# A two-block transformer kernel: order of splits, copy-outs, squares and gate in the second block's first projection

## What is computed

```python
h = rms_norm_2(x, norm_w[l]) * (1.0 + scale[:, None]) + shift[:, None]
proj = h @ w_in[l]
(qa, ka, va, za, beta_in, a_in, qb, kb, vb, zb, ga, gb) = jnp.split(proj, split_points, axis=-1)
qkv = causal_dwconv_silu(jnp.concatenate([qa, ka, va], axis=-1), conv_w[l])   # 4 taps
qa, ka, va = jnp.split(qkv, [DN_QK_WIDTH, 2 * DN_QK_WIDTH], axis=-1)
q_dn = l2_normalize(qa.reshape(b, s, DN_HEADS, DN_DK))       # x * rsqrt(sum(x*x) + EPS)
k_dn = l2_normalize(ka.reshape(b, s, DN_HEADS, DN_DK))
v_dn = va.reshape(b, s, DN_HEADS, DN_DV).astype(jnp.float32)
beta = jax.nn.sigmoid(beta_in.astype(jnp.float32))
g = -jnp.exp(a_log[l]) * jax.nn.softplus(a_in + dt_bias[l])
...
```

## Time and profile before

| | us |
|---|---|
| median of 3 runs | 2798.96 |
| lowest, highest | 2794.41, 2801.51 |
| span of the profiled execution | 2791.1 |
| TensorE busy in it | 2607.1 (93%) |
| VectorE busy | 1670.5 (60%) |
| ScalarE busy | 998.7 (36%) |
| GpSimd busy | 86.6 (3%) |

### The profile page before, as it was taken

One profiled execution on the slowest core, in us unless ns is written; L12 is line 12 of the kernel. 1 busy time (PEld: TensorE's weight loads), 2 busy tenths in 40 slices (PEclk: granted clock), 3 DMA queues, 4 the chain that ended last, 5 costly groups with the idle time before them and its releaser, 6 DMA issues. The chain is left out here.

```text
span 2791.1 us, 37630 instructions
## 1 busy us (share of the span) xinstructions
PE 2607.1 (93%) x15345; PEld 2208.5 (79%) x15345; DVE 1670.5 (60%) x2721; ACT 998.7 (36%) x1376; POOL 86.6 (3%) x132
## 2 busy tenths in 40 slices
PE   7999988999999999988999999989888898989997
PEld 3888877888888888856689989867778886777786
DVE  4888784467777766444447657566655653444644
ACT  4226545332212232344443323235422222334632
POOL 0100000000000000000000000021000000000000
PEclk9999999999999999999999999999989999999999
DMA  6650002223343323111034444212200000212232
GB/s 238 191 160 16 17 15 76 91 84 95 103 152 112 105 95 109 52 65 38 1 105 131 153 128 127 99 53 76 86 16 16 16 9 16 91 56 75 79 102 83
DMA packets 62109, 232.40 MB, mean 83 GB/s; under 512 B 6897, under 2 KB 9585, under 8 KB 61298
## 3 DMA queue, kind: packets, MB, share of 16 engines
q1 hardware_dynamic: 46962, 175.46, 19.1%
q0 software_dynamic: 14976, 54.53, 6.2%
HBM read 227.08 MB, written 2.10 MB: 82 GB/s over the span
## 5 line engine op out<-in xcount | busy, mean ns | idle before, releaser
L378 DVE TENSOR_TENSOR w_lo<-w_raw,w_hi 128x1024 fp32r<-128x1024 f32 (+4 forms) x284 | 348.8, 1228 | 381.8 <-ACT w_hi L337 379.2
L337 ACT ACTIVATE w_hi<-w_raw 128x1024 fp32r<-128x1024 f32 (+4 forms) x284 | 297.8, 1049 | 223.4 <-PE late_acc L459 93.4
L459 PE MATMUL mid_acc<-mid_h_hi,w_hi 128*128 128x258 f32 x832 | 279.5, 336 | 1.5 <-DVE mid_od_fq L627 1.0
L459 PE MATMUL mid_acc<-mid_h_hi,w_lo 128*128 128x258 f32 x832 | 279.0, 335 | 0.0
L459 PE MATMUL mid_acc<-mid_h_lo,w_hi 128*128 128x258 f32 x832 | 277.2, 333 | 0.0
L459 PE MATMUL late_acc<-late_h_hi,w_hi 128*128 128x258 f32 x704 | 199.3, 283 | 0.0
L459 PE MATMUL late_acc<-late_h_hi,w_lo 128*128 128x258 f32 x704 | 198.5, 282 | 0.0
L459 PE MATMUL late_acc<-late_h_lo,w_hi 128*128 128x258 f32 x704 | 197.7, 281 | 0.0
L459 PEld LDWEIGHTS mid_acc<-mid_h_hi,w_hi 128*128 128x128 f32 x832 | 157.3, 189 | 19.3 <-issue 2.4
L459 PEld LDWEIGHTS mid_acc<-mid_h_lo,w_hi 128*128 128x128 f32 x832 | 157.6, 189 | 18.6 <-issue 1.2
L459 PEld LDWEIGHTS mid_acc<-mid_h_hi,w_lo 128*128 128x128 f32 x832 | 156.9, 189 | 16.1
(11 more groups left out here) (558 smaller groups left out, 6271.1 us busy)
## 6 DMA issues: line engine op xcount, KB each, us to landing
w_raw<-in_up SPq DMA_DIRECT2D x88, 512.0 KB, 3.5
mid_side_raw<-in_ada_t POOLq DMA_DIRECT2D x48, 512.0 KB, 3.8
w_raw<-in_down SPq DMA_DIRECT2D x32, 704.0 KB, 4.0
qvz_side_raw<-in_ada_t POOLq DMA_DIRECT2D x32, 512.0 KB, 3.8
w_raw<-in_dn_qkv SPq DMA_DIRECT2D x25, 512.0 KB, 3.2
late_side_raw<-in_ada_t POOLq DMA_DIRECT2D x24, 512.0 KB, 4.0
w_raw<-in_da SPq DMA_DIRECT2D x18, 512.0 KB, 3.3
w_raw<-in_ev_qvz SPq DMA_DIRECT2D x16, 512.0 KB, 3.6
```

Of the source, the lines that this page charges most:

```text
L337: nc.scalar.activation(K.whi[:, g % 2, 0:width], K.raw[:, g % 2, 0:width], ACT.Copy).then_inc(K.hi_done, 1)
L378: nc.vector.tensor_tensor(K.wlo[:, g % 2, 0:width], K.raw[:, g % 2, 0:width], K.whi[:, g % 2, 0:width].bitcast(F32), ALU.subtract).then_in ...
L459: last = nc.tensor.matmul(self.acc[i % len(self.acc)][:, at:at + width], left[:, j, cols], right[k][:, moving:moving + width], start=(k == ...
```

## The change

The weight split moves from turn 1 to turn 0 of a tile, ahead of the copy-out (`take`, turn 0 to 1) on ScalarE and of the convolution (turn 0 to 1) on VectorE. The silu of a tile moves from its turn 5 to turn 2 of the next tile, that of the last tile to its turn 7. Sums and roots are scheduled one tile later, and the sums of slots 1 and others 2 turns earlier within it. GpSimd does the squares and, in pairs behind squares 6, 7, 10, 11, 14 and 15, also multiplies the slots by their roots, one slot (512 elements) at a time, the last four at the end; VectorE's multiplications of four slots are gone. The gate's steps on GpSimd follow squares 8, 9, 12 and 13. The gate's Exp and Ln on ScalarE stand right behind the first and second block of roots and use their table set; the reciprocal on VectorE is replaced by Exp(-Ln) on ScalarE; the gate's transposes move to tile 18.

```diff
--- before.py
+++ after.py
@@ -2554,9 +2554,10 @@
         self.ps = c.enter_context(nc.psum_tensor("dq_ps", [P, self.Q * LAT], F32))
         self.ps_t = c.enter_context(nc.psum_tensor("dq_ps_t", [P, LAT], F32))
         self.unread = c.enter_context(nc.psum_tensor("dq_unread", [P, 512], F32))[:, 0:P]
-        self.flow = Flow(K, c, "dq", w, 25, DT, h_hi, h_lo, 0, LAT, [(0, self.take), (5, self.silu)],
-                         [(0, self.convolve)], nxt, "conv0 conv1 conv2 conv3 silu_done", acc=acc,
-                         ready=ready)
+        self.flow = Flow(K, c, "dq", w, 25, DT, h_hi, h_lo, 0, LAT,
+                         [(1, self.take), (2, self.silu_before), (7, self.silu_last)],
+                         [(1, self.convolve)], nxt, "conv0 conv1 conv2 conv3 silu_done", acc=acc,
+                         ready=ready, split_turn=0)
         (self.padded, self.squared, self.total, self.logged, self.rooted, self.normed) = K.signals(
             "l2", "padded squared total logged rooted normed")
         (self.shifted, self.folded, self.tail, self.up, self.back, self.lost, self.inv, self.kept, self.ln_up,
@@ -2583,6 +2584,14 @@
         if i:
             act.wait_ge(conv3, i)
             self.nc.scalar.activation(self.dst[:, i - 1, :], self.conv[:, i % 2, :], ACT.Silu).then_inc(silu_done, 1)
+
+    def silu_before(self, act, f, i):
+        if i:
+            self.silu(act, f, i - 1)
+
+    def silu_last(self, act, f, i):
+        if i == f.n - 1:
+            self.silu(act, f, i)
 
     def convolve(self, dve, f, i):
         steps, silu_done = f.more[0:4], f.more[4]
@@ -2604,33 +2613,49 @@
     def sum_times(self):
 
 
-        return [(i + 3) * DT + (12 if i % self.Q == 0 and i else 9 if i % self.Q == 1 else 6) for i in range(16)]
+        return [(i + 4) * DT + (12 if i % self.Q == 0 and i else 7 if i % self.Q == 1 else 4) for i in range(16)]
 
     def root_times(self):
 
-        return [(i + 4) * DT + at for i in range(self.Q - 1, 16, self.Q) for at in (1.7, 12)]
+        return [(i + 5) * DT + 2.5 for i in range(self.Q - 1, 16, self.Q)]
 
     def norm_pool(self, pool):
-        nc, silu_done = self.nc, self.flow.more[4]
-        for i in range(16):
+        nc, Q, silu_done = self.nc, self.Q, self.flow.more[4]
+        gates = self.gates_pool(pool)
+
+        def square(i):
             pool.wait_ge(silu_done, i + 1)
             if i >= 2:
                 pool.wait_ge(self.total, i - 1)
             nc.gpsimd.tensor_tensor(self.sq[:, i % 2, :], self.dst[:, i, :], self.dst[:, i, :],
                                     ALU.mult).then_inc(self.squared, 1)
 
+        def normed(i):
+            pool.wait_ge(self.rooted, i // Q + 1)
+            nc.gpsimd.tensor_tensor(self.dst[:, i, :], self.dst[:, i, :], self.roots[:, i % Q, :],
+                                    ALU.mult).then_inc(self.normed, 1)
+        for i in range(16):
+            square(i)
+            if i >= 6 and i % Q in (2, 3):
+                first = i // Q * Q - Q + 2 * (i % Q - 2)
+                normed(first)
+                normed(first + 1)
+            elif i >= 8:
+                next(gates, None)
+        for i in range(16 - Q, 16):
+            normed(i)
+
     def norm_act(self, act):
         nc, Q = self.nc, self.Q
         for b in range(16 // Q):
             act.wait_ge(self.total, (b + 1) * Q)
             if b:
-                act.wait_ge(self.normed, b)
+                act.wait_ge(self.normed, b * Q)
             self.K.log_and_exp()
             nc.scalar.activation(self.roots[:, :, :], self.ps[:, :].rearrange("p (q t) -> p q t", q=Q), ACT.Ln,
                                  bias=self.K.eps[:, 0:1]).then_inc(self.logged, 1)
             act.wait_ge(self.logged, b + 1)
             nc.scalar.activation(self.roots[:, :, :], self.roots[:, :, :], ACT.Exp, scale=-0.5).then_inc(self.rooted, 1)
-            yield
             yield
 
     def norm_pe(self, pe):
@@ -2643,16 +2668,7 @@
                              start=True, stop=True).then_inc(self.total, 1)
             yield
 
-    def norm_dve(self, dve):
-        nc, Q = self.nc, self.Q
-        for b in range(16 // Q):
-            yield
-            dve.wait_ge(self.rooted, b + 1)
-            tiles = self.dst[:, b * Q:(b + 1) * Q, :]
-            nc.vector.tensor_tensor(tiles, tiles, self.roots[:, :, :], ALU.mult).then_inc(self.normed, 1)
-            yield
-
-    GATE_TIMES = (8.6, 13.6, 19.2, 26.6, 44.4, 48.4)
+    GATE_TIMES = (10.6, 66.6, 98.6, 148, 152)
 
     def gates_pool(self, pool):
         nc, H, z, e_log, ab = self.nc, DN_HEADS, self.z, self.e_log, self.ab
@@ -2660,22 +2676,25 @@
         nc.gpsimd.tensor_scalar(e_log[:, 1:2], e_log[:, 0:1], -1.0, None, ALU.mult).then_inc(self.neg_rate, 1)
         pool.wait_ge(self.tail, 1)
         nc.gpsimd.tensor_scalar(z[:, 2, :], z[:, 1, :], 1.0, None, ALU.add).then_inc(self.up, 1)
+        yield
         pool.wait_ge(self.up, 1)
         nc.gpsimd.tensor_scalar(z[:, 3, :], z[:, 2, :], -1.0, None, ALU.add).then_inc(self.back, 1)
         pool.wait_ge(self.back, 1)
         nc.gpsimd.tensor_tensor(z[:, 3, :], z[:, 1, :], z[:, 3, :], ALU.subtract).then_inc(self.lost, 1)
+        yield
         pool.wait_ge(self.inv, 1)
         pool.wait_ge(self.lost, 1)
         nc.gpsimd.tensor_tensor(z[:, 3, :], z[:, 3, :], z[:, 4, :], ALU.mult).then_inc(self.kept, 1)
         pool.wait_ge(self.pos, 1)
         pool.wait_ge(self.kept, 1)
         nc.gpsimd.tensor_tensor(z[:, 6, :], z[:, 6, :], z[:, 3, :], ALU.add).then_inc(self.soft, 1)
+        yield
         pool.wait_ge(self.soft, 1)
-        pool.wait_ge(self.ln_up, 1)
         nc.gpsimd.tensor_tensor(z[:, 6, :], z[:, 6, :], z[:, 5, :], ALU.add).then_inc(self.summed, 1)
         pool.wait_ge(self.neg_rate, 1)
         pool.wait_ge(self.summed, 1)
         nc.gpsimd.tensor_scalar(ab[0:H, :], z[:, 6, :], e_log[:, 1:2], None, ALU.mult).then_inc(self.g_done, 1)
+        yield
 
     def gates_dve(self, dve):
         nc, H, z, ab = self.nc, DN_HEADS, self.z, self.ab
@@ -2685,13 +2704,8 @@
         nc.vector.scalar_tensor_tensor(out=z[:, 1, :], in0=z[:, 0, :], scalar=-1.0, in1=z[:, 0, :],
                                        op0=ALU.mult, op1=ALU.min).then_inc(self.folded, 1)
         nc.vector.tensor_scalar(z[:, 6, :], z[:, 0, :], 0.0, None, ALU.max).then_inc(self.pos, 1)
-        yield
-        yield
-        dve.wait_ge(self.up, 1)
-        nc.vector.reciprocal(z[:, 4, :], z[:, 2, :]).then_inc(self.inv, 1)
-        yield
-        yield
-        yield
+        for _ in range(4):
+            yield
         dve.wait_ge(self.turned, 1)
         pv = self.ps_t[:, :].rearrange("p (c f) -> p c f", f=P)
         nc.vector.tensor_copy(self.by_token[:, :, 0:H], pv[:, :, 0:H])
@@ -2702,18 +2716,19 @@
         nc, H, z, ab = self.nc, DN_HEADS, self.z, self.ab
         act.wait_ge(*self.flow.freed(0))
         nc.scalar.activation(ab[32:32 + H, :], ab[32:32 + H, :], ACT.Sigmoid).then_inc(self.b_done, 1)
-        self.K.log_and_exp()
+        yield
         nc.scalar.activation(self.e_log[:, 0:1], self.a_log[0:H, :], ACT.Exp).then_inc(self.rate, 1)
-        yield
         act.wait_ge(self.folded, 1)
         nc.scalar.activation(z[:, 1, :], z[:, 1, :], ACT.Exp).then_inc(self.tail, 1)
         yield
         act.wait_ge(self.up, 1)
         nc.scalar.activation(z[:, 5, :], z[:, 2, :], ACT.Ln).then_inc(self.ln_up, 1)
+        act.wait_ge(self.ln_up, 1)
+        nc.scalar.activation(z[:, 4, :], z[:, 5, :], ACT.Exp, scale=-1.0).then_inc(self.inv, 1)
         yield
 
     def gates_pe(self, pe):
-        for _ in range(4):
+        for _ in range(3):
             yield
         pe.wait_ge(self.g_done, 1)
         pe.wait_ge(self.b_done, 1)
@@ -2735,7 +2750,6 @@
 
             @block.gpsimd
             def _(pool):
-                p.gates_pool(pool)
                 p.norm_pool(pool)
 
             @block.scalar
@@ -2746,7 +2760,7 @@
             @block.vector
             def _(dve):
                 norm.dve(dve)
-                weave(order, p.flow.dve(dve), iter(()), p.norm_dve(dve), p.gates_dve(dve))
+                weave(order, p.flow.dve(dve), iter(()), iter(()), p.gates_dve(dve))
 
             @block.tensor
             def _(pe):
```

## The result

| | before | after |
|---|---|---|
| median in us (runs) | 2798.73 (4) | 2780.07 (4) |
| lowest, highest | 2794.41, 2801.51 | 2778.37, 2781.27 |
| span of the profiled execution | 2791.1 | 2779.5 |
| first weight load of the stage to the start of its last matmul | 177.2 | 157.1 |

The medians are 18.7 us apart. The ratio, which is estimated from all executions and not from the two medians, is 0.9938, 95% interval 0.9924 to 0.9952: 17.4 us of 2798.73, 13.4 to 21.3. Timed again in five runs against 23 of before, it was 0.9932 (0.9920 to 0.9944). The forecast was 2777.5, range 2771 to 2791.

A forecast was written before the change was run, and what follows sets the result against it. TensorE, busy 93% of the span, was taken as the bound, with 21.8 us to win in this stage; less 0.3 allowed, 21.5 off the profiled 2791.1 gives 2769.6, plus 7.9 carried over is 2777.5 us, range 2771 to 2791.

The forecast's parts named there:

- What bounds it: In this stage TensorE, busy 93% of the span, bounds the kernel; 16.5 us gaps, 3.3 clock, 2.0 restarts can go.
- all that this change can win: 21.8 us: 167.9 between copy-outs of tiles 0 and 24, less 146.1 of TensorE's own work.
- Roots: First block of roots on ScalarE: w_lo(10) done at 10.4 us, wanted at 12.7; gaps of 1.91 to 2.43 go.
- Gate: GpSimd's gate chain no longer precedes the squares: the 7.08 us gap before the first sum and the clock's fall go.
- Turn-taking: VectorE and GpSimd exclude each other: each GpSimd instruction costs VectorE 0.85 to 0.89 us, 1.29 at most.
- The allowance of 0.3 us: Loss allowed for all late splits on VectorE: 0.3 us, bounds 0 to 3; w_lo(23) put 0.3 late.
- four tight places: Places where VectorE, beside GpSimd's squares and multiplications, has little slack: 0.9 us to spare early, 0.3 late in the last block.
- The silu's move: Silu goes behind the next tile's copy-out: ScalarE no longer waits 2 us for it, and nothing on TensorE needs it.
- The 7.9 us: Difference of the runs' median, 2798.96, from the profiled span, carried over from 2769.6 to the forecast 2777.5.
- (b): Rival: VectorE-GpSimd exclusion costs 1.29 us or more apiece, four places gap, 11 of 21.8 us come back; 2788, chance 0.18.
- (c): Rival: VectorE keeps GpSimd out, sums wait in TensorE's queue for squares 6, 10, 14; net gain 3 us, 2796, chance 0.10.
- (d): Rival, slower: one GpSimd instruction keeps VectorE off longer; all gain gone at 2.06 us, 2804 at 2.3; chance 0.06.

## Why the prediction was right, and where not

- **What bounds it.** Right. The profile before gave the 16.5 us of gaps, two falls of the clock and 21.8 us to win between the ends of tiles 0 and 24; the kernel with the multiplications on VectorE, which has no gap left behind tile 0, won 22.6 in the whole stage (177.46, the mean of the two profiles of before, to 154.85). That is 0.8 more than "all that this change can win". TensorE's own work was put a little too high: from the start of tile 1 to that of the last matmul the kernel without gaps takes 145.5 us, for 146.1, since the four transposes cost 0.46 us (tile 18, with one sum and them, 6.81 against 6.35) where 0.9 was allowed. One slip in the yardstick: the copy-out of tile 0 now stands behind a split and comes 1.0 us later, so the 146.7 us between copy-outs that the trace of after shows (146 forecast) are 147.7 between the ends of the tiles.
- **Roots.** The sum put w_lo(10) at 10.4 us behind the end of tile 7, wanted at 12.7; the trace has it 10.2 us behind. No gap there. Right in place and size.
- **Gate.** The first sum no longer waits, right. The prediction's terms for it are 7.08 of gap and 1.75 of clock, 8.8 us; the expectations put it at 7.5 + 1.8 = 9.3. With the turns of after in place it is 8.5 (163.3 to 154.8, multiplications on VectorE) or 6.1 (163.2 to 157.1, on GpSimd).
- **Turn-taking.** 0.85 to 0.89 us a GpSimd instruction was said to come from three rows; two show it, the third shows 0.39 (0.88 for 0.49). The runs give 0.90 and 0.94. The rule of the Trainium skill ("SBUF — State Buffer", "Who interferes with whom", on the shared port) agrees in kind; by its wording, the whole instruction, an estimate from the square that ran 1.04 us alone would be 1.04.
- **The allowance of 0.3 us was the term that was too small**: 2.2 us were lost. The prediction named four tight places. Of these, the last block's cost 0.2 us at tile 22 and 1.3 at tile 23, exactly the split that was put 0.3 late: it ended 0.8 us later than the sum had it (17.4 us behind the end of tile 19, for 16.6), since the convolution beside four multiplications took 1.51 + 4.15. Tile 17's 0.7 us falls in the round where the gate's third step, two two-input instructions, stands on GpSimd behind square 12; the sum had looked at the first round and the first step only. The kernel with the gate first, whose GpSimd has no gate steps there, begins tile 17 on time, so the 0.7 us are the gate step's beside multiplications; so does the kernel with these steps but the multiplications on VectorE. At tile 23 the kernel with the gate first still waits 0.4 us (0.8 from weight load to weight load).
- **The silu's move got no price and was a large part of the change.** The prediction said that ScalarE no longer waits 2 us for it, and that "nothing on TensorE needs it". That was true of its result, not of its place: it is ScalarE's queue that it holds, and the next split stands in it. With sums and roots behind it the move is worth 8.1 us on top of the order of splits (171.4 to 163.3), and the kernel without it loses 16.2 of 20.1 us. The forecast came out all the same since it worked out the whole kernel with every part in place; part by part it would have gone wrong, as the expectation for the order of splits alone did (12 to 13 us against 6 in the stage and 2 in the time).
- **From the stage to the median.** The forecast took 21.5 us off. The stage gave 20.2 (177.24 to 157.08): 1.9 less for the gaps above the allowance, 0.6 more for TensorE's own work. The medians moved by 18.7 and 18.6, inside the interval of 20.2. The forecast of 2777.5 is 2.6 under the measured 2780.07: 1.3 of it is the stage, and 1.5 lies outside it, where executions differ by more than that (the median of before moved by 0.2 the other way); that part is chance as far as the runs show. The 7.9 us that were carried over from the profiled span did no harm, since the sum is the median less 21.5, but they are no overhead: span and time of one execution are 1.8 us apart in every run, and the other 6.1 say that the profiled execution of before ran short outside the stage.
- **Rivals.** (b), the upper price of turn-taking, fell by 0.90. (c), a sum that waits for GpSimd: no such wait in after, though with 16 two-input instructions more one of 1.0 us appears. (d), slower: it decides at 2.06 us an instruction, the price being 0.90; with 16 two-input instructions more on GpSimd, 12.9 us came back and the kernel was still not slower than before. Table loads: 1.28 us and the next instruction right behind (1894.72, 1896.01), as the trace of before had it.

| kernel | stage, us | ratio (95% interval) |
|---|---|---|
| before | 177.2, 177.7 | 1 |
| order of splits alone | 171.4 | 0.9995 (0.9987 to 1.0004) |
| gate alone | 172.6 | 0.9986 (0.9975 to 0.9997) |
| turns alone (splits first, silu and sums a tile later) | 163.3 | 0.9942 (0.9930 to 0.9955) |
| turns and gate, multiplications on VectorE | 154.8, 154.8 | 0.9919, 0.9915 |
| after | 157.1, 157.1 | 0.9938, 0.9932 |
| after, silu in its own tile | 173.3 | 0.9982 (0.9970 to 0.9994) |
| after, splits second | 174.6 | 0.9981 (0.9969 to 0.9993) |
| after, gate first | 163.2 | 0.9933 (0.9915 to 0.9951) |
| after, 16 two-input instructions more on GpSimd | 170.0 | 0.9977 (0.9965 to 0.9990) |
| after, 16 one-input instructions more on GpSimd | 163.4 | 0.9951 (0.9934 to 0.9967) |

## What to carry to other kernels

Where engines take their queues in order, look for the loop that an instruction closes, not only for who needs its result: a cheap step that waits for another engine, ahead of the one that feeds the bound, costs what the loop is longer than the bound's own pitch, in every turn (here 7.57 against 6.35 us beside GpSimd's work). Parts of such a change are not worth their sum (here 6 and 5 us in the stage alone, 20 together), so test by leaving one out of the whole as well as by adding one to nothing. And an idle engine is no free one if it takes turns with a busy one: multiply its instructions by the price that the rows show before handing it work. Here one instruction of four slots on the busy engine was cheaper for that engine than four short ones on the idle one.

## What was not expected

- A one-input instruction of GpSimd (128x512) cost VectorE 0.42 us beside its convolutions and splits, a two-input one 0.90 to 0.94, though both lasted 1.9 us on GpSimd.
- Four multiplications as one instruction of 2048 elements on VectorE (2.28 us) cost it less than the same on GpSimd in four instructions (3.6 us of VectorE's time), and no split came late for TensorE.
- The same 16 squares and the gate cost VectorE more in the new order: its convolutions and 24 splits take 57.1 + 31.2 + 13.1 = 101.4 us before and 62.2 + 31.9 + 18.6 = 112.7 with the new turns and VectorE's own multiplications. TensorE didn't wait for any of it.
- Executions differ by up to 5 us in the 1840 us ahead of this stage and by up to 12 us in the 780 behind it, over all fourteen profiles, whose kernels are alike there; the stage itself repeats within 0.5 us for one kernel. A change of 10 us is read from the stage, not from the difference of two spans.
